# Front pieces regrouped, exponents and a scaling moved, and the last conv norm streamed in a one-core transformer layer

## The reference

```python
h = rms_norm(x, g_pre_mix[l])
proj = jnp.einsum('bsd,dp->bsp', h, w_in[l])
hc, bg, cg, q, k, v = jnp.split(proj, 6, axis=-1)
y_conv = short_gated_conv(hc, bg, cg, w_conv[l])
y_attn = chunked_band_attention(q, k, v, rel_bias[l])
y = jnp.concatenate([group_rms_norm(y_conv, g_conv_out[l], CONV_GROUPS),
                     group_rms_norm(y_attn, g_attn_out[l], N_HEADS)], axis=-1)
y = jnp.einsum('bsm,md->bsd', y, w_out[l])
x = x + rms_norm(y, g_post_mix[l])
h = rms_norm(x, g_pre_ffn[l])
gate, up = jnp.split(jnp.einsum('bsd,df->bsf', h, w_ffn_in[l]), 2, axis=-1)
f = jnp.einsum('bsf,fd->bsd', jax.nn.silu(gate) * up, w_ffn_out[l])
x = x + rms_norm(f, g_post_ffn[l])
```

## Time and profile before

| | |
|---|---|
| median of 3 runs | 1097.38 us (1097.09 to 1097.58) |
| the profiled execution | 1097.21 us, its span 1095.3 us |
| mean granted clock of TensorE | 0.999 |
| TensorE busy | 1084.5 us, 99% of the span |
| VectorE busy | 790.7 us, 72% |
| ScalarE busy | 471.0 us, 43% |
| GpSimd busy | 154.5 us, 14% |

### The profile page before, as it was taken

The page is one execution under the profiler, slowest core; times in us unless marked ns, Lnnn a source line. Parts: engine busy times, 40 slices in busy tenths (PEclk is TensorE's granted clock), DMA queues, the critical chain, the costliest instruction groups (busy, mean ns, idle before and its releaser), DMA issues.

```text
span 1095.3 us, 15872 instructions
## 1 busy us (share of the span) xinstructions
PE 1084.5 (99%) x5569; PEld 899.7 (82%) x5569; DVE 790.7 (72%) x1244; ACT 471.0 (43%) x799; POOL 154.5 (14%) x256
## 2 busy tenths in 40 slices
PE   8999999999999999999999999999999999999997
PEld 7888888878888888888888888888888888888886
DVE  6878888656667666969787878777787786555584
ACT  6642243356657565633232323223232256444541
POOL 2400000001101232102202211221121110000030
PEclk9999999999999999999999999999999999999999
DMA  7332123460010633517446444643544699777631
GB/s 271 107 124 77 49 57 132 156 242 1 21 59 20 231 137 114 186 46 238 140 120 203 163 145 132 218 133 121 189 165 160 199 331 362 232 230 230 214 115 77
DMA packets 117334, 168.30 MB, mean 154 GB/s; under 512 B 7880, under 2 KB 73432, under 8 KB 117280
## 3 DMA queue, kind: packets, MB, share of 16 engines
q1 hardware_dynamic: 99648, 107.50, 30.5%
q0 software_dynamic: 16464, 55.89, 14.5%
q10 hardware_dynamic: 1168, 4.20, 1.0%
HBM read 121.65 MB, written 49.04 MB: 156 GB/s over the span
## 4 chain that ended last, share of the span: by engine, by line
PE 74%; DVE 1%; ACT 0%; issue 0%; DVEq 0%; POOL 0%; POOLq 0%
PE psum L1355 35%; PE psum L1382 19%; PE psum L1237 8%; PE psum L941 6%; PE psum L983 2%; PE psum L965 2%; PE psum L955 1%; PE psum L930 1%; PE psum L1074 0%; PE psum L973 0%; PE psum L991 0%; PE psum L1081 0%; ACT misc L1636 0%; DVE arena L2736 0%; ACT misc L1432 0%; ACT arena L1627 0%
## 5 line engine op out<-in xcount | busy, mean ns | idle before, releaser
L1355 PE MATMUL psum<-arena_r,ws 128*128 128x512 f32 x960 | 224.1, 389 | 0.0
L1355 PEld LDWEIGHTS psum<-arena_r,ws 128*128 128x128 f32 x960 | 180.2, 188 | 37.4
L1355 PE MATMUL psum<-hT,ws 128*128 128x512 f32 x720 | 169.9, 389 | 0.0
L1355 PEld LDWEIGHTS psum<-hT,ws 128*128 128x128 f32 x720 | 135.1, 188 | 28.0
L1382 PE MATMUL psum<-hT 128*128 128x512 f32 (+1 forms) x600 | 135.2, 385 | 0.0
L1382 PEld LDWEIGHTS psum<-hT 128*128 128x128 f32 x600 | 111.3, 188 | 22.5
L2545 DVE TENSOR_TENSOR misc<-misc,psum 128x512 f32<-128x512 f32 x100 | 68.5, 685 | 47.9 <-PE psum L1355 45.6
L941 PE MATMUL psum<-hT,ws 128*128 128x512 f32 (+1 forms) x432 | 95.9, 373 | 0.0
L1193 PE MATMUL psum<-arena_r,ws 128*128 128x512 f32 x372 | 86.9, 389 | 0.0
L1833 ACT ACTIVATE ws<-o_raw 128x512 fp32r<-128x512 f32 x40 | 25.1, 627 | 139.0 <-DVE o_raw L2523 138.5
L941 PEld LDWEIGHTS psum<-hT,ws 128*128 128x128 f32 x432 | 72.5, 189 | 13.9 <-issue 2.2
(11 more groups left out here) (273 smaller groups left out, 1566.6 us busy)
## 6 DMA issues: line engine op xcount, KB each, us to landing
raw<-in_w_ffn_in SPq DMA_DIRECT2D x44, 512.0 KB, 4.4
act_scratch<-arena POOLq DMA_DIRECT2D x77, 256.0 KB, 3.2
raw<-in_w_in SPq DMA_DIRECT2D x22, 512.0 KB, 4.0
arena<-in_w_ffn_out POOLq DMA_DIRECT2D x22, 512.0 KB, 5.7
arena<-act_scratch SPq DMA_DIRECT2D x38, 256.0 KB, 3.3
arena<-in_x SPq DMA_DIRECT2D x16, 512.0 KB, 5.6
raw<-in_w_out SPq DMA_DIRECT2D x16, 512.0 KB, 3.5
raw<-act_scratch SPq DMA_DIRECT2D x26, 256.0 KB, 3.4
```

What stands on the lines that cost most here:

```text
L1355: last = mm(blocks(bank), w[:, k * P:(k + 1) * P], b_operand(i, part, k), start=fresh_bank and k == 0 and w is hi and part == 0, stop=k == ...
```

## The change

It does five things.

- `FILLS` is changed. From pair 1 on no piece stands in step 0, and steps 2, 4 or 6 (step 1 in pair 2) have two. `fill` of step 2 moves on TensorE from ahead of the transposes of P to behind them. By the new lists half 1 ends in step 2 of pair 0, half 2 in step 1 of pair 1, half 6 in step 2 of pair 3; the others end where they did. The taps fall in step 2 and step 4 of pair 1 and step 4 of pair 2 (before: steps 3 and 5 of pair 1 and step 5 of pair 2), and chunk 2 is split one step earlier.
- ScalarE runs both exponents of step 3 ahead of the reading of P, as it did in steps 5 and 7. Its drain of step 2 moves behind the reading and the second exponent.
- VectorE's drain of step 1 moves behind the reading of o, and `o_scale` from step 4 to the end of step 3.
- The last conv row's norm is made as those of the other rows are: its squares are split in two parts (ScalarE after the attention, VectorE in the last step), four matmuls of 512 columns with a matrix of 1/64 give the means, already spread, inside the third chunk of the output projection; ScalarE takes the reciprocal root, and VectorE makes four passes over the row in the third to fifth chunk. The transposes of the last pair's o move from inside the fourth to inside the fifth chunk.
- The semaphores and functions that this makes needless are gone, GpSimd's power for the conv row among them.

```diff
+        same_head_last = misc_r[:, 2304:2304 + P]
+        SQ_HIGH, SQ_LOW = 10, 11
...
-        FILLS = [[1, 1, 1, 1, 1, 0, 1, 0, 1], [1, 1, 1, 1, 1, 0, 1, 0, 1], [1, 1, 1, 1, 1, 0, 1, 0, 1], [1, 2, 1, 1, 1, 0, 1, 0, 0]]
+        FILLS = [[1, 1, 2, 0, 1, 0, 1, 0, 1], [0, 1, 2, 0, 2, 0, 1, 0, 1], [0, 2, 1, 0, 1, 0, 2, 0, 1], [0, 1, 2, 0, 2, 0, 2, 0, 0]]
...
-            conv_norm_factors(PAIRS - 1)
...
-                if s in (1, 2, 8):
+                if s in (1, 8):
                     fill(t, s)
...
                 transpose_p(t, s - 1)
-                if s in (4, 6):
+                if s in (2, 4, 6):
                     fill(t, s)
...
+            def means(bank, heads, high, low):
+
+                for half in range(2):
+                    for part in (high, low):
+                        last = mm(bank[:, half * HALF:(half + 1) * HALF], heads, row_r(part)[:, half * HALF:(half + 1) * HALF],
+                                  start=(part == high), stop=(part == low))
+                last.then_inc(conv_stat, 1)
...
             def transpose_last_o():
-                pe.wait_ge(conv_var, 1)
+                pe.wait_ge(mix_read, 1)
                 transpose_o(PAIRS, PP[3])
+
+            def last_means():
+                for half in range(2):
+                    pe.wait_ge(half_free[half], OUT0)
+                pe.wait_ge(tile_free, PAIRS * NT + 1)
+                pe.wait_ge(conv_mixed, means_split(LAST))
+                means(PP[3], same_head_last, SQ_HIGH, SQ_LOW)
...
-            INSIDE = {3: transpose_last_o, 10: rows_inside(0), 13: rows_inside(2), 19: rows_inside(3)}
+            INSIDE = {2: last_means, 4: transpose_last_o, 10: rows_inside(0), 13: rows_inside(2), 19: rows_inside(3)}
...
-                if c == 2:
-                    for half in range(2):
-                        pe.wait_ge(half_free[half], OUT0)
-                    pe.wait_ge(tile_free, PAIRS * NT + 1)
-                    pe.wait_ge(conv_sq, squared(LAST, 0))
-                    conv_stats(PP[3]).then_inc(conv_stat, 1)
-                if c == 6:
-                    pe.wait_ge(oT_read, PAIRS)
-                    pe.wait_ge(conv_rs, 1)
-                    conv_norms(PP[3], 0, NT).then_inc(conv_norm, 1)
...
-                if s in (5, 7):
+                if s in (3, 5, 7):
                     exp(t, 2 * s + 1)
                 if more and s == 7:
                     high_k(t)
-                if s in (1, 2, 3, 8):
+                if s in (1, 3, 8):
                     drain(t, s)
                 if s > 0:
                     read_pT(t, s - 1)
-                if s < NT and s not in (5, 7):
+                if s < NT and s not in (3, 5, 7):
                     exp(t, 2 * s + 1)
-                if s in (4, 6):
+                if s in (2, 4, 6):
                     drain(t, s)
...
-            square_conv(LAST), square_pair(LAST)
+            square_conv(LAST)
+            act.wait_ge(o_psum, PAIRS * NT)
+            spread_heads(same_head_last)
+            act.wait_ge(conv_sq, squared(LAST, 0))
+            go(row_r(SQ_HIGH), row(CU), ACT.Copy).then_inc(conv_sq, 1)
+            square_pair(LAST)
...
-                if c == 4:
-                    act.wait_ge(oT_psum, PAIRS)
-                    spread_conv()
+                if c == 2:
+                    act.wait_ge(conv_stat, PAIRS)
+                    go(row(SQ_HIGH), PP[3], ACT.Abs_reciprocal_sqrt, bias=eps_col[:, 0:1]).then_inc(conv_root, 1)
...
-                if s in (1, 2, 3, 5, 7):
+                if s in (2, 3, 5, 7):
                     drain(t, s)
...
                 if s == 1 and t > 0:
                     read_o(t - 1, NT - 2)
+                if s == 1:
+                    drain(t, s)
                 if s == 2 and t > 0:
                     sum_squares(t)
                     o_norm(t)
                 if s == 4:
-                    if t > 0:
-                        o_scale(t)
                     read_o(t, 0)
...
+                if s == 3 and t > 0:
+                    o_scale(t)
...
                     split_out_w(2), split_out_a(2)
+                    low_sq(LAST, SQ_HIGH, SQ_LOW)
                     sum_squares(PAIRS)
...
-            def conv_last_stats():
-                dve.wait_ge(conv_stat, PAIRS)
-                ts(var[:, :], PP[3][:, 0:16], 1.0 / HD, EPS, ALU.mult, ALU.add).then_inc(conv_var, 1)
-
-            def conv_last(_):
-                dve.wait_ge(conv_norm, 1)
-                stt(row(PAIRS - 1), PP[3], params[:, LAST, 3:4], row(CV), ALU.mult, ALU.mult).then_inc(mix_done, 1)
+            def conv_last(part):
+                f, v = row(SQ_HIGH), row(CU)
+                if part == 0:
+                    dve.wait_ge(conv_root, PAIRS)
+                    stt(v, PP[3], EPS, f, ALU.add, ALU.mult).then_inc(mix_read, 1)
+                    return
+                if part == 1:
+                    dve.wait_ge(mix_read, 1)
+                    stt(v, v, -0.5, f, ALU.mult, ALU.mult).then_inc(mix_read, 1)
+                    return
+                dve.wait_ge(mix_read, 2)
+                chain(stt(f, v, 1.5, f, ALU.add, ALU.mult))
+                stt(row(PAIRS - 1), row(CONV_ROWS[LAST]), params[:, LAST, 3:4], f, ALU.mult, ALU.mult).then_inc(mix_done, 1)
                 dve.wait_ge(mix_done, 1)
...
-            tasks = {3: [(attn_last, 0)], 5: [(conv_last, 0)],
+            tasks = {3: [(conv_last, 0)], 4: [(attn_last, 0), (conv_last, 1)], 5: [(conv_last, 2)],
```

More of the change, by code:

```diff
@@ L473, in trunk_layer @@
         mix_done = sem("mix_done")
+        mix_read = sem("mix_read")
         a_hi = sem("a_hi")
@@ L1075, in transpose_o @@
                 last.then_inc(oT_psum, 1)
[L1077 to L1088, removed]
             def values(i, steps, part):
@@ L1202, in stats @@
                     pe.wait_ge(conv_mixed, mixed(t - 1))
-                for half in range(2):
[L1204 to L1207, removed]
+                means(PP[2], same_head, CR, CU)
             behind = {(4, 2): 0, (5, 1): 1, (5, 5): 2}
@@ L1544, in square_y, with spread_heads @@
                 go(row(CU), row(CONV_ROWS[t]), ACT.Square).then_inc(conv_sq, 1)
+            def spread_heads(to):
+                go(to.rearrange("p (g d) -> p g d", d=HD),
+                   group[:, :].rearrange("p (g o) -> p g o", o=1).broadcast_to([P, 2, HD]), ACT.Copy, scale=1.0 / HD)
             def high_sq(t):
@@ L1550, in high_sq @@
                     act.wait_ge(consts_made, 6)
[L1551 to L1552 removed]
+                    spread_heads(same_head)
                 if t > 0:
@@ L1560, in conv_roots @@
                 go(row(CR), bank, ACT.Abs_reciprocal_sqrt, bias=eps_col[:, 0:1]).then_inc(conv_root, 1)
-            def spread_conv():
-                act.wait_ge(conv_factors, 1)
-                go(row(CR).rearrange("p (g d) -> p g d", d=HD),
-                   crs[:, :].rearrange("p (g o) -> p g o", o=1).broadcast_to([P, 16, HD]), ACT.Copy
-                   ).then_inc(conv_rs, 1)
             scale = -HD ** -0.5
@@ L2106, in tap, with low_sq, mix_row @@
                     chain(stt(v[:, n:SEQ], u[:, 0:SEQ - n], w, v[:, n:SEQ], ALU.mult, ALU.add))
-            def low_sq(t):
+            def low_sq(t, high=CR, low=CU):
                 dve.wait_ge(conv_sq, squared(t, 1))
-                tt(row_r(CU), row(CU), row_r(CR).bitcast(F32), ALU.subtract).then_inc(conv_mixed, 1)
-            def mix_row(t):
-                f, mean, y = row(CR), PP[2], row(CONV_ROWS[t])
+                tt(row_r(low), row(CU), row_r(high).bitcast(F32), ALU.subtract).then_inc(conv_mixed, 1)
+            def mix_row(t, mean, f, out, done):
                 dve.wait_ge(conv_root, t + 1)
@@ L2118, in mix_row, with mix_front @@
                 chain(stt(f, mean, 1.5, f, ALU.add, ALU.mult))
-                stt(y, y, params[:, t, 3:4], f, ALU.mult, ALU.mult).then_inc(conv_mixed, 1)
+                stt(out, row(CONV_ROWS[t]), params[:, t, 3:4], f, ALU.mult, ALU.mult).then_inc(done, 1)
+            def mix_front(t):
+                mix_row(t, PP[2], row(CR), row(CONV_ROWS[t]), conv_mixed)
             def gated_round(n):
@@ L2182, in _ @@
             make_u3(4)
-            mix_row(0)
+            mix_front(0)
             dve.wait_ge(prod, multiplied(4, 3))
@@ L2199, in _ @@
                 if n == 5:
-                    mix_row(1)
+                    mix_front(1)
                 make_u3(n)
@@ L2216, in _ @@
                 if n == 5:
-                    mix_row(2)
+                    mix_front(2)
                 front_low(n + 1, 4), front_low(n + 1, 5)
```

9 lines of the change are left out of this document (removed).

## The result

The changed kernel takes 1101.05 us (median of eight executions, 1099.37 to 1102.25), the kernel before 1097.24 beside it: the ratio is 1.0035, with an interval of 1.0027 to 1.0044. It is slower by 3.8 us, where 2.8 was forecast. The profiled execution took 1101.89 us (span 1100.1) with a mean granted clock of 0.995. The eight are not alike: the one with clock 0.999 took 1099.37, four with 0.997 or 0.998 took 1100.81 to 1101.06, the three with 0.995 took 1101.89 to 1102.25.

The account below looks back on a forecast made before the run. TensorE, with work in flight for 99% of the span, was taken to bound the kernel. New waits of 6.7 less gains of 3.85 cost 2.85, so 1097.2 + 2.8 = 1100.0 us, range 1098.0 to 1102.0.

Parts of the forecast that it names:

- rival 2: Attention: later waits (0.8 and 0.2) are swallowed and joints may bring 0.5 more, giving 1098.3 us; chance 0.11.
- The drains, 4.2: Pairs 0 and 3: VectorE's step 2 drain delays the copy of o, so TensorE waits 1.3 and 2.9 in step 3.
- Rival 1: Pairs 0 and 3: the drains hide, so their 4.2 is nothing and the kernel takes 1095.8 us, faster; chance 0.09.
- Step 2's transposes, 1.5: Pairs 2 and 3: without the piece ahead, transposes of P wait 0.75 each for VectorE's reading of turned o.
- rival 3: Pair 3's wait: TensorE's clock falls to 1.2 GHz, costing 3 us more, 1103.0 us; chance 0.08.
- Gains of the exponents and the scaling, 1.4 and 0.3: Exponents first end step 4's wait of 0.34 in four pairs; the moved scaling ends pair 1's step 5 hole.
- The scaling's price, 0.8: Scaling ahead of step 4's biases, and pair 1's tap ahead of step 3's, delay TensorE; 0 to 1.6, taken as 0.8.
- The joints: Attention: 28 pieces in 20 places instead of 27 save 0.09 for each of seven joints, a gain of 0.6.
- the first step: With no piece there, the former pair's products wait 0 to 0.2 in each of three pairs; 0.2 in all.
- Conv, 1.55: Output stage: TensorE loses small matmuls and transposes of 1.68 and 0.87, gains four matmuls of 1.0; gain 1.55 (1.2 to 1.9).
- The load: Conv norm on ScalarE: root's table load of 1.28 hidden before the means; by the skill's price the sum is 0.4 higher.
- Chunk 2's split, nothing: Pair 0: the split one step earlier falls into idle time of ScalarE and VectorE and costs nothing.

Follow-up runs that it names:

- experiment 3: The kernel before with only the last conv norm streamed and VectorE's first-step drain moved behind the reading of o: 1095.15 us, ratio 0.9981.
- (5): experiment 3 with the exponents of step 3 first, the scaling still in step 4: 1094.53 us, ratio 0.9974.
- experiment 4: The changed kernel with the old lists of pieces and step 2's piece ahead of the transposes again: 1093.37 us, ratio 0.9965 to the kernel before.
- experiment 1: The changed kernel with VectorE's drain of step 2 issued in step 3, behind the copy of o: 1095.39 us, ratio 0.9984 to the kernel before.
- experiment 2: The changed kernel with twenty unused identity transposes on TensorE in pair 3's wait: 1099.23 us, ratio 1.0018 to the kernel before.
- experiment 6: experiment 1 with the pieces of step 2 put ahead of the transposes of P in pairs 2 and 3: 1095.45 us, ratio 0.9983 to the kernel before.
- experiment 8: experiment 1 with one piece of pair 3's step 2 on either side of the transposes of P: 1094.81 us, ratio 0.9979 to the kernel before.
- 7: experiment 6 with the scaling back in step 4: 1095.85 us, ratio 0.9990 to the kernel before.
- experiment 9: experiment 8 with chunk 2's split one step later in pair 0, where the kernel before had it: 1094.49 us, ratio 0.9975 to the kernel before.

## Why the prediction was right, and where it was not

The runs make a chain of medians, each step with its part:

| kernel | us | step |
|---|---|---|
| before (1097.2 to 1097.3) | 1097.25 | |
| conv streamed, the first-step drain moved (3) | 1095.15 | -2.1 |
| and exponents first (5) | 1094.53 | -0.6 |
| and scaling moved (4) | 1093.37 | -1.2 |
| and the new lists, without the drains' wait (1) | 1095.39 | +2.0 |
| and the drains' wait, clock kept (2) | 1099.23 | +3.8 |
| and the clock (after) | 1101.05 | +1.8 |

- **The sign and the time.** Forecast 1100.0 in 1098.0 to 1102.0, measured 1101.05. Without the clock the sum should have come out at 1099.2 (experiment 2), so its terms were 0.8 too high together, and the clock, priced at nothing in the sum, brought 1.8. That the time lies inside the range is in part luck: the range was to leave out a fall of the clock, which came, and the two misses offset each other in part. (The bounds of the terms, added up, give 1097.0 to 1102.6, and not the 1098.6 to 1101.4 that the prediction has; rival 2's deductions give 1098.5, not 1098.3.)
- **The drains, 4.2.** Right in place, mechanism and size: 1.3 and 2.8 in the trace against 1.3 and 2.9, and 3.8 between experiments 1 and 2. Rival 1 asked whether VectorE might come late to its drain; it stood idle 2.73 and 3.63 before it. One thing about the old place was wrong: in pair 3 the short read behind the drain did cost TensorE 0.2 (experiment 3), which the change takes away.
- **Step 2's transposes, 1.5.** Right: 0.78 in each pair, put down to VectorE's reading of turned o. What the prediction did not see is that the pieces' new place has its own work: they cover ScalarE's reading of P there (experiment 6). The loss comes from taking one of two covers, not from the order alone (experiment 8).
- **What the sum left out: the clock, at nothing.** The prediction had it as rival 3, at this place, for 3 us at most, with a chance of 0.08, though it noted that the wait was nearly as long as the idle time before the fall in the earlier trace rows. Rows of after show 2.9 in the profiled execution. By the times seven of eight lost 1.4 us or more to the one that did not, and the median lost 1.8. (The mean clocks alone tell less: executions of before have 0.998 too.) The Trainium skill, "TensorE: Matmul & The Clock Gate", section "Why this matters for your kernels", warned of a gap between bursts; the rows from 333 to 343 agree for a gap inside the kernel, here a wait of 2.6.
- **Gains of the exponents and the scaling, 1.4 and 0.3.** Together 1.8, near the 1.7 forecast, but split otherwise: 0.6 and 1.2. They were costed as if each stood alone. A gain on TensorE of 0.36 makes it arrive earlier at the next use of VectorE, and only the moved scaling lets it through.
- **The scaling's price, 0.8.** Mis-sized: about 0.3, in pair 2 alone, at the scores of step 5 rather than at the products; pair 1 shows none, and with the lists of before there is none at all (experiment 4).
- **The joints and the first step.** The first step cost 0.07 in each of three pairs, the 0.2 forecast. The joints were put at 0.6. The waits above (1.6 to 1.7, 0.3 and 0.2) make 2.1 to 2.2, and the profiled executions of experiments 1 and 4, 1095.11 and 1093.40, lie 1.7 apart, so 0.4 to 0.5 is left for the joints. The medians lie 2.0 apart, probably since some executions of experiment 1 also waited for chunk 2's weights.
- **Conv, 1.55.** Mis-sized, at its upper bound: the 2.1 of experiment 3 less the 0.2 of the moved drain, 1.9, of which rows show 1.64. The load was put ahead of the means, out of the way; in fact it began only as the means ended, and the root followed it at once. The Trainium skill, "ScalarE: Activation LUTs", section "What ACT_TABLE_LOAD costs", would have had 1.4 more at that place and so 0.4 on TensorE by the prediction's estimate; load to root measured 1.29, with 0.03 ahead of the load, and no such loss appeared.
- **Chunk 2's split, nothing.** True in after's profile, where the drain had already delayed the stage. Once that wait is gone it cost 1.4 in the profiled execution of experiment 8, 0.5 in those of 6 and 7 and nothing in that of 1; with the split a step later nothing is left of it (experiment 9). The prediction counted the engines' idle time for the moved split, and not whether its weights had landed by then.

## What to carry to other kernels

An instruction that waits for another engine is costed by what stands behind it in its own queue: behind VectorE's drain stood the copy that TensorE needed, and moving the drain behind that copy gave 5.7 us, 1.8 of it the clock's. When filler work is moved, ask what it covered at its old place and what it covers at the new one, and look at each place that wants cover by itself. When a step moves earlier, ask also whether the data that it reads have landed, and be suspicious of a cover that is itself a wait about to be removed.

## What the runs showed of the hardware

- In the profiled execution a wait of 2.6 us inside a busy stretch took the granted clock from 1.00 to 0.50, and it was whole again only in the stretch from 343 on, 7 us after the wait's end; the cost after the wait, 2.9, was larger than the wait's own 2.6. Beside the wait of 1.12 in pair 0 it read 1.00. It was not the same in every execution: one of eight kept 0.999 and took 1099.37, as with the clock kept.
- The spread of a kernel's times can name the cause. With TensorE kept busy through the wait it went from 2.9 to 0.2 us, and with the weights landed in time from 2.04 to 0.43.
